# Layer 1's grouped attention steps: value products ahead of the next pair's probability transposes

## The reference

```python
def block_attention(q, k, v):
    ...
    def one_block(qi):
        sc = jnp.einsum('bqhgd,bkhd->bhgqk', qi, kf) * scale
        p = jax.nn.softmax(sc, axis=-1)
        return jnp.einsum('bhgqk,bkhd->bqhgd', p, vf)
```

## Time and profile before

| | us |
|---|---|
| median of 3 runs | 1137.41 (1137.26 to 1137.61) |
| the profiled execution | 1137.43 |
| its span, first to last instruction | 1135.6 |
| PE busy | 1120.5 (99%) |
| DVE busy | 734.0 (65%) |
| POOL busy | 589.3 (52%) |
| ACT busy | 517.0 (46%) |

### The profile page before, as it was taken

The page is one execution under the profiler, slowest core; times in us unless marked ns, Lnnn a source line. Parts: engine busy times, 40 slices in busy tenths (PEclk is TensorE's granted clock), DMA queues, the critical chain, the costliest instruction groups (busy, mean ns, idle before and its releaser), DMA issues.

```text
span 1135.6 us, 18725 instructions
## 1 busy us (share of the span) xinstructions
PE 1120.5 (99%) x6288; PEld 928.1 (82%) x6288; DVE 734.0 (65%) x1418; ACT 517.0 (46%) x948; POOL 589.3 (52%) x791
## 2 busy tenths in 40 slices
PE   9999999999999999999999999999999999999998
PEld 6796667998888888888899866799888888888887
DVE  4788697568766778677579787766773144412445
ACT  5637775354422443134444588545442244323442
POOL 3553444535555554555648445354565455555554
PEclk9999999999999999999999999999999999999999
DMA  9946521224455354543424320221532323223212
GB/s 372 353 155 194 197 76 60 95 89 159 178 182 185 131 183 167 204 167 134 142 82 138 120 68 20 70 87 53 179 133 93 98 94 104 93 93 100 83 58 75
DMA packets 44456, 149.45 MB, mean 132 GB/s; under 512 B 5344, under 2 KB 7008, under 8 KB 44256
## 3 DMA queue, kind: packets, MB, share of 16 engines
q1 hardware_dynamic: 43808, 148.17, 37.7%
q10 hardware_dynamic: 576, 0.36, 0.1%
HBM read 144.32 MB, written 2.10 MB: 129 GB/s over the span
## 4 chain that ended last, share of the span: by engine, by line
PE 52%; issue 18%; POOL 15%; POOLq 6%; DVE 4%; ACT 2%; DMA 1%; DVEq 1%; ACTq 0%; SPq 0%
POOL w_lo L658 15%; PE ps L777 14%; PE ps L783 14%; PE ps L778 14%; POOLq L660 5%; PE ps L1095 3%; PE ps L1109 2%; PE ps L1128 2%; DVE prob L2144 1%; DMA w_raw<-w_slots 1%; DVE nmx L2120 1%; PE ps L1160 1%; DVE ada_prod L1692 1%; DVEq L2143 0%; ACT prob L1601 0%
## 5 line engine op out<-in xcount | busy, mean ns | idle before, releaser
L658 POOL TENSOR_TENSOR w_lo<-w_raw,w_hi 128x256 fp32r<-128x256 f32 (+3 forms) x694 | 524.3, 786 | 431.2 <-ACT w_hi L1372 414.7
L777 PE MATMUL ps<-h_hi,w_hi 128*128 128x512 f32 (+1 forms) x832 | 307.6, 370 | 2.0 <-POOLq L661 1.1
L778 PE MATMUL ps<-h_lo,w_hi 128*128 128x512 f32 (+1 forms) x832 | 306.7, 369 | 0.0
L783 PE MATMUL ps<-h_hi,w_lo 128*128 128x512 f32 (+1 forms) x832 | 306.6, 369 | 0.0
L1372 ACT CAST w_hi<-w_raw 128x1024 fp32r<-128x1024 f32 (+2 forms) x169 | 173.0, 1028 | 189.3 <-PE ps L777 186.1
L2223 DVE SCALAR_TENSOR_TENSOR u_sb<-ps,par,u_sb 128x510 f32<-128x510 f32 x176 | 131.8, 749 | 102.5 <-ACT u_sb L1644 89.0
L777 PEld LDWEIGHTS ps<-h_hi,w_hi 128*128 128x128 f32 x832 | 156.8, 188 | 29.1 <-DVE h_lo L1779 1.6
L778 PEld LDWEIGHTS ps<-h_lo,w_hi 128*128 128x128 f32 x832 | 156.8, 188 | 26.3
L783 PEld LDWEIGHTS ps<-h_hi,w_lo 128*128 128x128 f32 x832 | 156.8, 188 | 26.1
L777 PE MATMUL ps<-a_hi,w_hi 128*128 128x512 f32 (+1 forms) x400 | 145.7, 364 | 0.0
L778 PE MATMUL ps<-a_lo,w_hi 128*128 128x512 f32 (+1 forms) x400 | 145.4, 364 | 0.0
(11 more groups left out here) (217 smaller groups left out, 1549.5 us busy)
## 6 DMA issues: line engine op xcount, KB each, us to landing
w_raw<-w_slots SPq DMA_DIRECT2D x152, 512.0 KB, 3.6
ada_raw<-ada_slots SPq DMA_DIRECT2D x88, 512.0 KB, 4.3
w_raw<-w_slots SPq DMA_DIRECT2D x16, 384.0 KB, 3.0
first_raw<-first_slots SPq DMA_DIRECT2D x8, 512.0 KB, 13.3
w_raw<-w_slots SPq DMA_DIRECT2D x8, 416.0 KB, 4.7
x<-x_t SPq DMA_DIRECT2D x4, 512.0 KB, 5.5
qr<-q_rot SPq DMA_DIRECT2D x16, 128.0 KB, 4.1
c_all<-c_wide SPq DMA_DIRECT2D x1, 1024.0 KB, 13.3
```

The lines of the kernel that those rows point to most:

```text
L658: nc.gpsimd.tensor_tensor(w_lo[:, j, c], w_raw[:, j, c], w_hi[:, j, c].bitcast(F32), ALU.subtract)
L777: hh = mm(out, stat[0], mov[0], start=first, stop=False)
L778: hl = mm(out, stat[0], mov[1], start=False, stop=False)
L783: return mm(out, stat[1], mov[0], start=False, stop=last)
```

## The change

In the loop over steps of layer 1 (L > 0), for steps 3 to NA + 2 = 10, TensorE's outputs(i-3) is written ahead of prob_transposes(i-2) instead of behind it. Layer 0, the later steps, and every other engine's list are as they were. The waits inside the two functions are unchanged.

```diff
@@ -1191,9 +1191,11 @@
                     if i == NP + 1:
                         out_part(L, 0, (1,))
                         group_sums(1)
+                    if L > 0 and 3 <= i < NA + 3:
+                        outputs(i - 3)
                     if 0 <= i - 2 < NP:
                         prob_transposes(i - 2)
-                    if 0 <= i - 3:
+                    if 0 <= i - 3 and not (L > 0 and i < NA + 3):
                         outputs(i - 3) if i < NP + 2 else None
                     if L == 0 and 0 <= i - 1 < 4 * len(STREAMED):
                         stream_products(i - 1)
```

## The result

The changed kernel takes 1152.61 us (median of 4 runs, 1151.57 to 1154.13), the kernel before 1137.51 (1137.26 to 1138.18). The ratio is 1.0129, with a 95% interval of 1.0117 to 1.0141: 15.1 us slower, where 11.7 were forecast, and 1.1 us above the upper end of the range. The direction and the ring came out as forecast; two further costs, a wait for POOL and falls of TensorE's clock, were not in the sum.

A forecast was written before the change was run, and what follows sets the result against it. TensorE, busy 99% of the span, was taken to bound the kernel. Seven serial turns of 5.31 us with entry and exit gave 11.7 us over 1137.4, so 1149.1 us, range 1146.5 to 1151.5.

The forecast's parts named there:

- the ring: Layer 1, changed steps: copy o_t, outputs, transposes, copy prob_t, four exponentials, next copy o_t run serially, 5.31 us a step.
- TensorE's time is the kernel's time: Whole kernel: TensorE busy 99% of 1135.6 us; idle added midway is paid in full, only 1.3 us later idle.
- outputs takes `o_done` along: Changed steps: outputs(i-3) waits for pair i-4's copy o_t, behind step i-1's exponentials; transposes now queue behind it too.
- 5.31 us a turn: Layer 1's changed steps: links 1.02, 1.11, 0.91, 1.81 and 0.46 sum to 5.31 us a step, replacing 3.70.
- Start of the ring: Step 3: outputs(0) waits for bank 7, starting at 660.25; transposes of pair 1 start at 661.27 instead of 659.73.
- The sum for the ring, 11.7: Through step 10 and exit: transposes of pair 8 are 12.4 us late, then outputs(8) 11.7 us late.
- From there the steps are as before: After outputs(8): later steps unchanged, every row 11.7 us later to the end.
- rival (a): TensorE's clock falls in the changed stretch, doubling outputs and transposes: 14 us more, 1163 us; chance 0.05.
- A granted clock below 1.00 in the stretch: Layer 1's changed stretch: a granted TensorE clock under 1.00 there would show the forecast wrong.
- crowding: Changed steps: exponentials and the copy stretch where other engines crowd them, up to another 0.9 us on the upper bound.
- (b): Changed steps: delay paid once, ScalarE's 2.7 us of waiting absorbs later turns; 1140.1 us; chance 0.05.
- (c): Changed steps: outputs fills the transposes' 0.9 us wait for scaled rows, not slower; 1136.5 us; chance 0.03.

The follow-up runs named there:

- copy_ahead: Changed kernel, but ScalarE makes its copy o_t ahead of the four exponentials of the same step instead of behind them: 1139.0 us, ratio 1.0004 to the kernel before.
- two_copies: Changed kernel with ScalarE's copy o_t made twice in each of layer 1's eight grouped pairs: 1158.54 us, 20.4 over the kernel before.
- again: The changed kernel run once more with a profile, no edit: 1152.94 us, ratio 1.0132 to the kernel before.
- filler: Changed kernel plus six unused 128x128 matmuls on TensorE ahead of outputs in steps 4, 6 and 7 of layer 1: 1151.37 us, ratio 1.0113 to the kernel before.
- filler_sums_later: Changed kernel with six unused matmuls in steps 4, 6, 7, and layer 1's group_sums(0) moved behind scores(12): 1149.94 us, 11.72 over the kernel before.
- steps_3_7: Changed order in steps 3 to 7 alone, the kernel before's order in steps 8 to 10: 1146.64 us, ratio 1.008 to the kernel before.
- steps_8_10: Changed order in steps 8 to 10 alone, otherwise the kernel before: 1142.37 us, ratio 1.0039 to the kernel before.

## Why the prediction was right or wrong

- *TensorE's time is the kernel's time, nothing later gives it back.* Right. Behind the stretch the waits for DVE and POOL at L777 are 0.9 us together after and 1.1 before; the spans differ by what the stretch and its start account for, 16.7.
- *outputs takes `o_done` along and closes a ring.* Right, and shown by copy_ahead (cut: 0.8 us over before) and two_copies (a link made longer: the turn longer by the same).
- *5.31 us a turn.* Right: 5.30 or 5.31 in every turn without a fall of the clock, in six traces (this kernel's, again, filler, filler_sums_later, steps_3_7, steps_8_10).
- *Start of the ring.* Right but for a trifle: outputs(0) to outputs(1) was forecast 5.31 and is 5.31. outputs(0) starts 1.05 us behind the fill, not the 1.01 forecast.
- *The sum for the ring, 11.7.* Right: 11.74 in the trace, 11.72 as the difference of medians of filler_sums_later (9.6 to 13.1).
- *Exit: "From there the steps are as before."* Wrong. I followed the ring out on TensorE and ScalarE and left POOL out, whose squares of pair 7 stand between the copy o_t and group_sums(0). Before, the group sums started 2.15 us after that copy (689.89 to 692.04), and the value products of pair 8 lay in between. Now these wait for the copy themselves, so they and the squares start together, and the squares take longer: term missed, 1.3 to 1.4 us. POOL's addition took 1.51 us here and 0.73 before, because it now starts inside DVE's scaling, as far as the rows show it (no run moves the two apart): that is 0.8 of the 1.4, and with an addition of 0.73 the wait would have been some 0.6 (an estimate from the same rows).
- *The clock, rival (a), 0.05.* Mis-sized in chance and in form. I took it as all or nothing, 14 us, and weighed it by a stretch in which the idle was spread (12 to 20 us, 7.1 of 8 busy). What happens is in between: some of the three idle stretches of 2.1 us bring a fall, each worth 0.55 to 1.35 us of ring. That is 3.1 us in the profiled execution, 1.2 in again's, 1.57 between the medians of again and filler. The earlier trace rows showed the clock at 1.00 at least until 1132, 1.9 us into the final idle; that didn't allow me to hold 2.1 us safe. A granted clock below 1.00 in the stretch was named as a sign of being wrong, and it came.
- *The range.* Its upper side had 0.9 for crowding that didn't come and half a microsecond for the unknown. The two terms above, 1.4 and about 1.6, add to 3.0, and 1149.1 + 3.0 = 1152.1 is the measured median within half a microsecond. (With the half microsecond added, its lower end comes to 1146.4, not 1146.5.)
- *Rivals (b) and (c).* Both refuted, (b) by steps_3_7 and steps_8_10, (c) by the waits. Under (c) I read 0.6 us as outputs waiting for the copy; the earlier trace rows has it for the weight loads (PEld), and in the list of PE's own waits of the kernel before outputs does not appear.

So two steps of the prediction failed: the exit was taken to hold no further wait, and the clock was put at nothing in the sum. They measured 1.4 and about 1.6 us.

The Trainium skill (TensorE: Matmul & The Clock Gate, section "Why this matters for your kernels") warns of idle gaps between bursts of matmuls, but of longer ones than these, so by it they would have been safe. The measurement decides: of the twelve gaps of 1.9 to 2.6 us in four traces (this kernel's, again, steps_3_7, two_copies) eight were followed by a fall, and of those of 0.25 to 1.7 us none. Whether transposes count as busy in the way that matmuls do (its section "Part 4: PE-mode transpose") is not settled by these runs: the filler matmuls changed the idle time and the share of matmuls together.

## What to carry to other kernels

Before moving an instruction ahead of another, list the waits that it brings along and ask on which engine, and behind what, the instruction stands that ends each of them. If that one is queued behind work that waits for what you have just pushed back, you have closed a ring, and its turn is the plain sum of its links: add them up from start-to-start distances, and count the turns. Then follow the last turn out on every engine, the slow helper too, and ask how long the engine that used to be full now stands still, since its clock may fall.

## What the hardware showed that was not expected

- The granted clock went to 0.50 behind single idle stretches of 1.9 to 2.6 us, in a program whose TensorE is 98% busy over the whole (75% from 655 to 705 us in again), and not always: in the profiled execution behind all three, in again behind one of three, in steps_3_7 and two_copies behind two of three. Idle of 0.25 to 1.7 us (the 1.55 of step 5 in again and the 1.71 of two_copies among it) never brought a fall in these traces. In the profiled execution of the changed kernel each fall began only after the matmuls had resumed (idle until 666.1, the clock still 1.00 in the window that ends at 667.11), so the slow rows can begin later than the one behind the gap; in two_copies both began ahead of the matmuls, by 0.1 and 0.6 us.
- Doing 1.6 us of useless matmuls three times made the kernel 1.57 us faster (again against filler, medians of four runs each, whose ranges don't meet).
- A POOL instruction that takes 0.73 us at other places takes up to 1.5 when it starts inside DVE's scaling of the rows, and the scaling takes 1.42 to 1.56 us in place of 1.22 to 1.23 where it starts inside one of POOL's (both kernels). By the estimate above this cost TensorE 0.8 us, through a helper that is 51% busy.
